# Gathering all rows first, and three 2 MB weight transfers per expert block instead of six of 1 MB

## The chip, the core and the metric

The kernel runs on one NeuronCore of a Trainium2 chip. The metric is the device time of one execution in microseconds (us). The core has five engines: TensorE (PE: matrix products, which accumulate in PSUM), VectorE (DVE), ScalarE (ACT), GpSimd (POOL) and SyncE (SP, which issues most transfers). They run side by side and wait for each other through semaphores. Sixteen DMA engines move data between HBM and the on-chip memory SBUF.

## The reference

One encoder block on 512 tokens of 1024 features, all in float32: a mixing part (differential attention, a conformer convolution, gates, an output projection) and then a mixture of experts. Only the second part changes:

```python
def hier_moe(h, w_rg, b_rg, w_re, b_re, w_g, w_u, w_d):
    # top-1 group of 8, then the top 2 of its 8 experts, for each of N = 512 tokens
    ...
    def expert_block(args):
        xb, e = args          # a block of rows that chose expert e
        return (jax.nn.silu(xb @ w_g[e]) * (xb @ w_u[e])) @ w_d[e]
    ...                       # weighted, summed into the tokens' rows
```

There are 64 experts. Each has w_g and w_u of 1024 x 512 and w_d of 512 x 1024, 2 MB apiece, so 6 MB of weights stand behind every block of rows. The 1024 choices (512 tokens, 2 each) are few beside that.

## The kernel before

The mixing part and the router take the first 420 us or so. After them the kernel runs one block of up to 64 rows after another (`BLK = 64`). Blocks 0 and 1 (`AHEAD = 2`) are written out and belong to experts 0 and 1, whose weights are loaded early; the rest is a loop whose count is read from `count_i`. With these inputs 62 blocks run, 60 of them in the loop.

A block works like this. `gather()` (L1382) picks the rows of the block: a one-hot matrix that DVE makes (`next_onehot`, L1098 to L1101) is multiplied with the normalized tokens `h2`, four tiles of 128 tokens, two matmuls each. DVE copies the result to `rows_sb` (L1120), PE transposes it (`transpose_rows`, L1389), and DVE copies it to `hTb` (L1122), the block's input. `block_products` (L1405) then multiplies it with gate and up weights in two halves of eight matmuls; the output's two halves of 64 partitions are computed side by side. ACT applies silu (L765), DVE multiplies (L1117), PE transposes the product (L1417), ACT copies it (L767), and PE multiplies it with the down weights in two halves of four matmuls (L1426). ACT copies the result to `y_sb` (L773) and POOL scatters it to HBM (L579).

The order is written out by hand. While block b is multiplied, block b + 1 is gathered: tiles 0 and 1 between the halves of gate and up, tile 2 behind them, tile 3 behind the transposes of the product, the transposes of the rows between the halves of down. So every one of the 62 blocks carries a whole gather.

The weights lie in two sets of six places of 1 MB (`weights`). Block b uses set b % 2. SP issues `load_sixth` (L487) in the order gate and up of half 0, gate and up of half 1, down half 0, down half 1. In the loop it waits, for each sixth, until PE has used what lies there (`gu_used` counts halves of gate and up, `down_used` counts blocks), and until the same sixth of the block before has landed (`in_w`). So at most one transfer of each sixth is under way. A run is what one partition takes in one piece of contiguous HBM: 8 KB for gate and up (four rows of 512), 4 KB for down (one row of 1024).

After the last block DVE reads the scattered rows back, adds them with their weights and normalizes, about 28 us.

## Time and profile before

| | us |
|---|---|
| median of 3 runs | 1401.41 (1401.35 to 1402.8) |
| the profiled execution | 1401.0 |
| its span, first to last instruction | 1399.2 |

| engine | busy us | share of the span |
|---|---|---|
| PE (matmul) | 1327.6 | 95% |
| DVE | 431.9 | 31% |
| ACT | 209.4 | 15% |
| POOL | 186.3 | 13% |

The transfers moved 435.78 MB, and SP's queue was busy for 76.1% of the time of 16 engines. Over the block loop, the last two thirds of the span, the page's slices show PE at nine tenths or more and the DMA engines at nine tenths or more with 413 to 418 GB/s. The profiled execution lies 1.8 us above its span and 0.4 us under the median. A share of busy time says which engine worked, not which one the others waited for; for that the waits and the order of time are needed. In the timelines an fp32 matmul shows as two records, so eight matmuls read x16.

### The profile page before, as it was taken

The page shows a single profiled execution, that of the slowest core. Times are in us where ns is not written, and L with a number is a line of the kernel's source. Part 1 is how long each engine was busy: PE and PEld are TensorE (multiplying, and loading weights), DVE is VectorE, ACT ScalarE, POOL GpSimd, SP SyncE. Part 2 cuts the span into 40 slices and gives each one's busy share as a digit, 9 for nine tenths or more (in the row PEclk, how much of TensorE's full clock was granted, in tenths as well). Part 3 has the DMA queues.
Part 4 walks back from the last instruction along what each step waited for, and adds up shares of the span by engine and source line. Part 5 has one row for each costly group of instructions (what it writes and reads, how often), then busy time and mean ns, then how long its engine had stood idle before and what let it go on. Part 6 is the DMA issues. An engine that isn't in the chain of part 4 may idle for free.

```text
span 1399.2 us, 17476 instructions
## 1 busy us (share of the span) xinstructions
PE 1327.6 (95%) x5883; PEld 580.5 (41%) x5883; DVE 431.9 (31%) x843; ACT 209.4 (15%) x453; POOL 186.3 (13%) x244
## 2 busy tenths in 40 slices
PE   5999988999979999999999999999999999999991
PEld 3878766744453333333333333333333333333330
DVE  4799344342334221121121122122112112112214
ACT  3232324430110100100000000010010000000002
POOL 2355433000000001001001001000100100100100
PEclk9999999999978999999999999999999999999996
DMA  5331311116145999999999999999999999999984
GB/s 208 115 121 61 121 60 57 68 57 251 49 180 219 386 417 416 417 417 417 416 418 417 415 417 417 415 416 417 416 417 417 413 414 410 415 414 415 416 339 186
DMA packets 93090, 435.78 MB, mean 311 GB/s; under 512 B 13488, under 2 KB 13517, under 8 KB 60810
## 3 DMA queue, kind: packets, MB, share of 16 engines
q1 hardware_dynamic: 86896, 429.23, 76.1%
q0 software_dynamic: 5312, 5.28, 1.2%
q10 hardware_dynamic: 858, 0.95, 0.2%
q8 instruction: 15, 0.25, 0.1%
q14 instruction: 9, 0.07, 0.0%
HBM read 429.10 MB, written 18.36 MB: 320 GB/s over the span
## 4 chain that ended last, share of the span: by engine, by line
issue 78%; PE 13%; POOL 2%; DVE 2%; DMA 2%; POOLq 1%; ACT 1%; ACTq 0%; DVEq 0%
PE ps_proj L1193 10%; PE ps_proj L1234 2%; POOL sb_tick L578 1%; POOL sb_tick L589 1%; DVE sb_x L1142 1%; DMA sb_weights<-in_w_in 1%; DMA sb_rb_sb<-in_rel_bias 1%; PE ps_scores L1248 1%; POOL expert_rows L579 0%; DVE sb_x L1152 0%; DVE sb_conv L932 0%; DMA sb_weights<-expert_rows 0%; POOL sb_weights_r L557 0%; PE ps_proj L1216 0%; PE ps_proj L1225 0%
## 5 line engine op out<-in xcount | busy, mean ns | idle before, releaser
L1405 PE MATMUL ps_proj<-sb_weights,sb_scratch 128*64 128x512 f32 x1984 | 446.9, 592 | 0.8 <-DVE sb_scratch L1107 0.8
L1405 PEld LDWEIGHTS ps_proj<-sb_weights,sb_scratch 128*64 128x64 f32 x1984 | 142.3, 137 | 283.2 <-issue 271.8
L1382 PE MATMUL ps_proj<-sb_hT,sb_scratch 128*64 128x512 f32 x1008 | 254.0, 605 | 0.0
L1426 PE MATMUL ps_scores<-sb_weights,sb_scratch 128*64 128x512 f32 x992 | 237.0, 598 | 0.0
L1117 DVE TENSOR_TENSOR sb_scratch<-sb_scratch,ps_proj 128x256 f32<-128x256 f32 x62 | 26.1, 421 | 536.0 <-ACT sb_scratch L765 536.0
L578 POOL TENSOR_TENSOR sb_tick<-sb_tick 1x1 f32<-1x1 f32 x62 | 11.6, 187 | 1013.9 <-ACT sb_scratch L773 1013.9
L1193 PE MATMUL ps_proj<-sb_hT_r,sb_weights_r 128*128 128x512 f32 x512 | 126.9, 401 | 2.7 <-POOL sb_weights_r L557 2.7
L1382 PEld LDWEIGHTS ps_proj<-sb_hT,sb_scratch 128*64 128x64 f32 x1008 | 67.4, 138 | 120.5 <-issue 120.5
L1426 PEld LDWEIGHTS ps_scores<-sb_weights,sb_scratch 128*64 128x64 f32 x992 | 65.3, 136 | 116.9 <-issue 90.3
L1193 PEld LDWEIGHTS ps_proj<-sb_hT_r,sb_weights_r 128*128 128x128 f32 x512 | 96.8, 192 | 30.5 <-issue 10.1
L765 ACT ACTIVATE sb_scratch<-ps_proj 128x256 f32<-128x256 f32 x62 | 23.8, 385 | 492.1 <-PE ps_proj L1405 492.1
L557 POOL TENSOR_TENSOR sb_weights_r<-sb_weights,sb_weights_r 128x1024 fp32r<-128x1024 f32 x36 | 86.0, 2404 | 76.4 <-ACT sb_weights_r L640 75.4
L773 ACT ACTIVATE sb_scratch<-ps_scores 128x512 f32 (+1 forms) x62 | 37.0, 598 | 318.6 <-PE ps_scores L1426 311.0
L1122 DVE COPY sb_scratch<-ps_proj 128x512 f32<-128x512 f32 x62 | 42.9, 692 | 99.5 <-PE ps_proj L1389 99.5
L1120 DVE COPY sb_scratch<-ps_proj 128x512 f32<-128x512 f32 x62 | 42.9, 691 | 96.1 <-PE ps_proj L1382 96.1
L579 POOL DMA_INDIRECT expert_rows<-sb_scratch,sb_idx x62 | 61.4, 991 | 32.3 <-issue 31.9
L1193 PE MATMUL ps_proj<-sb_x_r,sb_weights_r 128*128 128x512 f32 x256 | 63.2, 389 | 0.0
L1341 PE MATMUL ps_proj<-sb_weights 128*128 128x512 f32 x128 | 55.6, 593 | 0.0
L1193 PEld LDWEIGHTS ps_proj<-sb_x_r,sb_weights_r 128*128 128x128 f32 x256 | 48.1, 188 | 10.0
L1389 PEld LDWEIGHTS ps_proj<-sb_consts,sb_scratch 128*128 128x128 f32 x252 | 26.6, 142 | 52.1 <-issue 50.3
L1098 DVE TENSOR_TENSOR sb_scratch<-sb_small,sb_consts 128x512 f32<-128x512 f32 x62 | 43.0, 693 | 7.6 <-issue 1.2
L845 DVE SCALAR_TENSOR_TENSOR ps_scores<-sb_pad,sb_taps,ps_scores 128x512 f32<-128x512 f32 x58 | 42.5, 752 | 0.9
(221 smaller groups left out, 811.1 us busy)
## 6 DMA issues: line engine op xcount, KB each, us to landing
sb_weights<-in_w_exp_down SPq DMA_DIRECT2D x124, 1024.0 KB, 13.8
sb_weights<-in_w_exp_gate SPq DMA_DIRECT2D x124, 1024.0 KB, 14.0
sb_weights<-in_w_exp_up SPq DMA_DIRECT2D x124, 1024.0 KB, 15.2
sb_weights<-in_w_in SPq DMA_DIRECT2D x9, 2048.0 KB, 7.9
sb_x<-in_x SPq DMA_DIRECT2D x8, 512.0 KB, 9.2
sb_weights<-in_w_out SPq DMA_DIRECT2D x2, 2048.0 KB, 10.5
sb_weights<-expert_rows SPq DMA_DIRECT2D x4, 1024.0 KB, 7.9
sb_weights<-in_w_conv_pw SPq DMA_DIRECT2D x1, 2048.0 KB, 7.7
```

The source lines that it names most:

```text
L557: pool.tensor_tensor(w_low[name][:, :, j * P:(j + 1) * P], raw, high.bitcast(F32), ALU.subtract).then_inc(w_split, 1)
L579: pool.indirect_dma_start(out=y_dram, out_offset=bass.IndirectOffsetOnAxis(ap=idx[:, parity:parity + 1], axis=0), in_=y_sb[:, parity, :], ...
L773: act_e.activation(y_sb[:, of_parity(b), :].rearrange("p a s -> p (a s)"), ps_y, ACT.Copy)\
L845: dve.scalar_tensor_tensor(out=dst, in0=pad[:, c, k:k + SEQ], scalar=taps[:, c, k:k + 1], in1=conv_sum[c], op0=ALU.mult, op1=ALU.add).then ...
L1098: dve.tensor_tensor(hot_k, over(dest, BLK), pos8, ALU.is_equal).then_inc(loop_v, 1)
L1120: dve.tensor_copy(rows_sb, ps_rows[:, :]).then_inc(rows_ready, 1)
L1122: dve.tensor_copy(hTb, ps_hTb[:, :].rearrange("p (c s) -> p c s", s=P)).then_inc(hTb_ready, 1)
L1193: last = mm(dst[:, :], w[:, c, :], rows[:, c, :], start=i + c == 0, stop=i == 2 and c == KD - 1)
L1341: last = mm(dst[:, :], gates[:, c, t * P:(t + 1) * P], w[:, c, :], start=c == 0, stop=c == KD - 1)
L1382: last = mm(ps_rows[g * BLK:(g + 1) * BLK, :], onehot[:, t, :], h2[:, t, g * NW:(g + 1) * NW], start=t == 0, stop=t == T - 1)
L1405: last = mm(ps_gu[g * BLK:(g + 1) * BLK, :].rearrange("p (a n) -> p a n", a=2), hTb[:, c, half * BLK:(half + 1) * BLK], weights[:, place(p ...
L1426: last = mm(ps_y[g * BLK:(g + 1) * BLK, :], actT[:, j, half * BLK:(half + 1) * BLK], weights[:, place(parity, 4 + half), 2 * j + g, :], st ...
```

## The change

Three things change.

**Gathering.** The 1024 choices are gathered once, in expert order, in pieces of 64 that need not end where an expert's block ends: 16 pieces for the choices that are not in blocks 0 and 1's first 64 rows. They are written to a new buffer `hTs`, and block b takes its input as a slice of it from a position that DVE loads from `start_i`. Only the first 16 blocks carry a gather (`block_with_gather`, `GATHERED = 14` of them in the loop); all later ones (`block_products`) carry none. `sorted_places()` computes the positions in the first block: 18 more instructions on DVE and 2 more on PE (`rest_of_experts`).

**Order.** In a block with a gather, the piece's tiles are spread differently, the last two between the halves of gate and up, and the first two of the next piece later in the block.

**Weights.** `load_third` issues gate, up and down whole, 2 MB each: runs of 16 KB for gate and up, 8 KB for down. Each waits for both halves of gate and up, or for the block, to be used. The product's transposes read every second column, to fit the new order of down's rows. The buffers v_sb, conv, strip and pad become one tensor `work`, over which `hTs` lies.

```diff
-            def load_sixth(b, i, e):
-                dst = weights[:, place(b, i), :, :]
...
+            wd = ap("w_exp_down")[0].rearrange("e (h p j) n -> e p h (j n)", h=2, p=P)
+
+            def load_third(b, i, e):
+
+                dst = weights[:, place(b, 2 * i, 2), :, :]
+                if i < 2:
+                    sp.dma_start(dst.rearrange("p a c n -> p (a c n)"),
+                                 (wg, wu)[i][e].rearrange("e p n -> (e p) n")).then_inc(in_w[i], 16)
...
-                for sixth in range(6):
-                    if sixth in (0, 2):
-                        sp.wait_ge(gu_used, 2 * i + 1 + sixth // 2)
-                    if sixth == 4:
+                for third in range(3):
+                    if third == 0:
+                        sp.wait_ge(gu_used, 2 * i + 2)
+                    if third == 2:
                         sp.wait_ge(down_used, i + 1)
...
+            def rows_to_sorted(n, at):
+                dve.wait_ge(hTb_done, n)
+                dve.tensor_copy(hTs[:, at].rearrange("p (s g c) -> p c g s", g=2, c=4),
+                                ps_hTb[:, :].rearrange("p (c g s) -> p c g s", c=4, g=2)).then_inc(hTs_ready, 1)
+
+            def sorted_to_block(start):
+                dve.tensor_copy(hTb.rearrange("p c (g s) -> p c g s", g=2),
+                                hTs[:, bass.ds(start, BLK * KD)].rearrange("p (s g c) -> p c g s", g=2, c=4))\
+                    .then_inc(hTb_ready, 1)
...
+            dve.wait_ge(rows_done, 1)
+            block_onehot()
+            sorted_places()
+            prepare_slots()
+            gate_and_up(0)
+            copy_rows(2)
+            rows_to_block(2)
+            take_slots()
+            list_rows(0, slots[:, 0:1])
+
+            def block_with_gather(b, at, start, block_slots):
+                copy_rows(b + 2)
+                next_onehot(2 * b + 4, 2 * b + 5)
+                gate_and_up(b)
+                rows_to_sorted(b + 2, at)
+                dve.wait_ge(hTs_ready, b)
+                sorted_to_block(dve.value_load(start, min_val=0, max_val=2 * SEQ * KD))
+                list_rows(b, block_slots)
...
+            def first_block():
+                pe.wait_ge(hTb_ready, 1)
+                gate_up_half(0, 0, 0)
+                rest_of_experts()
+                pe.wait_ge(hot_b, 2)
+                gather([0, 1])
+                gate_up_half(0, 0, 1)
+                gather([2])
+                transpose_act(0)
+                gather([3])
+                pe.wait_ge(actT_ready, 1)
+                down_half(0, 0, 0)
+                pe.wait_ge(rows_ready, 2)
+                transpose_rows()
+                down_half(0, 0, 1)
+                slot_rows()
+                pe.wait_ge(hot_b, 3)
+                gather([0, 1])
```

The queue of SP in its loop, before (names are those of the code; `in_w0` to `in_w5` count landings of the six sixths):

```order
L522 ISA [waits gu_used]
L487 REGISTER_ALU [waits in_w0]
L487 DMA sb_weights<-in_w_exp_gate 128x2048
L487 ISA [waits in_w1]
L487 DMA sb_weights<-in_w_exp_up 128x2048
...
L487 ISA [waits in_w2,gu_used]
...
L487 ISA [waits in_w4,down_used]
L487 DMA sb_weights<-in_w_exp_down 128x2x1024
```

and of the change:

```order
L527 ISA [waits gu_used]
L493 REGISTER_ALU [waits in_w0]
...
L493 DMA sb_weights<-in_w_exp_gate 128x4096
L493 ISA [waits in_w1]
L493 DMA sb_weights<-in_w_exp_up 128x4096
...
L496 ISA [waits in_w2,down_used]
L496 DMA sb_weights<-in_w_exp_down 128x2x2048
```

Six transfers became three of twice the size, and one wait for half of gate and up is gone: the first of them now stands behind the whole.

PE in its loop, one block, before:

```order
L1405 MATMUL ps_proj<-sb_weights,sb_scratch 64x512 [waits in_w1,in_w0]
L1405 MATMUL ps_proj<-sb_weights,sb_scratch 64x512 x7
...
L1382 MATMUL ps_proj<-sb_hT,sb_scratch 64x512 [waits hot_b]
L1382 MATMUL ps_proj<-sb_hT,sb_scratch 64x512 x3
L1405 MATMUL ps_proj<-sb_weights,sb_scratch 64x512 [waits in_w3,in_w2]
...
L1382 MATMUL ps_proj<-sb_hT,sb_scratch 64x512 x2
L1417 MATMUL ps_aT<-sb_consts,sb_scratch 128x128 [waits act_ready]
...
L1426 MATMUL ps_scores<-sb_weights,sb_scratch 64x512 [waits in_w4,actT_ready]
...
L1389 MATMUL ps_proj<-sb_consts,sb_scratch 128x128 [waits rows_ready]
```

and one block of the change's second loop:

```order
L1480 ISA [waits hTb_ready]
L1484 MATMUL ps_proj<-sb_weights,sb_scratch 64x512 [waits in_w1,in_w0]
L1484 MATMUL ps_proj<-sb_weights,sb_scratch 64x512 x15
L1493 MATMUL ps_aT<-sb_consts,sb_scratch 128x128 [waits act_ready]
L1493 MATMUL ps_aT<-sb_consts,sb_scratch 128x128
L1501 MATMUL ps_scores<-sb_weights,sb_scratch 64x512 [waits in_w2,actT_ready]
L1501 MATMUL ps_scores<-sb_weights,sb_scratch 64x512 x7
```

The eight matmuls of the gather (L1382) and the four transposes (L1389) are gone from the block; nothing stands any more between the product's chain and what waits for it.

DVE in the first block of the change, between the one-hot (L1132) and the multiplication that the product's transposes wait for (L1162):

```order
L1132 TENSOR_TENSOR sb_scratch<-sb_scratch 128x256 [waits loop_v]
L1069 TENSOR_SCALAR sb_work<-sb_consts,sb_work 64x1
...
L1078 COPY sb_work<-ps_oT 128x64 [waits rest_done]
...
L1091 CAST sb_start_i<-ps_aT 1x80 [waits starts_done]
L1096 TENSOR_SCALAR sb_work<-sb_work 128x8 [waits link_v]
...
L1105 COPY sb_work<-sb_work 128x8x64 [waits link_v]
L1162 TENSOR_TENSOR sb_scratch<-sb_scratch,ps_proj 128x256 [waits gsig_ready]
```

Before, the rows from L1096 on (`prepare_slots`) followed the one-hot directly. The rows of `sorted_places`, L1069 to L1091, now stand ahead of them.

## Rows read from the trace of the kernel before

**Rows 1.** Timeline (start, us, engine, instructions): PE over one block.

```profile
810.65 3.60 PE L1405 MATMUL ps_proj<-sb_weights,sb_scratch 128*64 128x512 f32 x16
...
815.80 3.60 PE L1405 MATMUL ps_proj<-sb_weights,sb_scratch 128*64 128x512 f32 x16
...
820.34 0.44 PE L1417 MATMUL ps_aT<-sb_consts,sb_scratch 128*128 128x128 f32 x2
...
821.62 1.89 PE L1426 MATMUL ps_scores<-sb_weights,sb_scratch 128*64 128x512 f32 x8
...
823.44 0.66 PE L1389 MATMUL ps_proj<-sb_consts,sb_scratch 128*128 128x128 f32 x4
...
824.03 1.94 PE L1426 MATMUL ps_scores<-sb_weights,sb_scratch 128*64 128x512 f32 x8
...
825.79 3.60 PE L1405 MATMUL ps_proj<-sb_weights,sb_scratch 128*64 128x512 f32 x16
```

**Rows 2.** Windows: busy us of PE, PEld, DVE, ACT, POOL; clock, DMA share, GB/s.

```profile
480.00:1000.00 520.00, 517.20 (x2406) 172.97 (x2404) 103.87 (x238) 46.44 (x102) 46.49 (x104) 1.00 1.02 416
1000.00:1340.00 340.00, 338.11 (x1574) 113.11 (x1572) 69.17 (x159) 30.82 (x68) 29.73 (x66) 1.00 1.02 415
```

**Rows 3.** Waits of SP's queue, 480 to 780 us (total us, times, longest).

```profile
SPq L487 <- PE ps_scores L1426: 95.7, 19, 5.3
```

**Rows 4.** The same view, 1000 to 1350 us.

```profile
SPq L487 <- DMA sb_weights<-in_w_exp_up: 84.1, 45, 2.2
```

**Rows 5.** Timeline of SP's queue: two issues of the down weights, 22 blocks apart.

```profile
1007.94 2.70 SPq L487 DMA_DIRECT2D sb_weights<-in_w_exp_down  x2
...
1347.93 2.97 SPq L487 DMA_DIRECT2D sb_weights<-in_w_exp_down  x2
```

**Rows 6.** Windows in stretches of one run length, the columns of rows 2.

```profile
119.00:123.00 4.00, 4.00 (x19) 3.33 (x18) 4.00 (x7) 0.45 (x1) 0.00 (x0) 1.00 1.03 390
...
334.00:343.00 9.00, 9.00 (x22) 3.99 (x21) 2.29 (x4) 0.00 (x0) 0.00 (x0) 1.00 1.02 409
343.00:348.00 5.00, 5.00 (x13) 2.24 (x12) 0.69 (x1) 0.00 (x0) 0.00 (x0) 1.00 1.03 424
...
1378.00:1387.00 9.00, 0.00 (x0) 0.00 (x0) 6.54 (x6) 3.95 (x7) 0.00 (x0) 0.50 1.01 427
```

**Rows 7.** Timeline of PE: the end of block 0 and the start of block 1.

```profile
439.64 0.44 PE L1417 MATMUL ps_aT<-sb_consts,sb_scratch 128*128 128x128 f32 x2
...
445.19 2.01 PE L1375 MATMUL ps_scores<-sb_conv,sb_v_sb 128*128 128x80 f32 x16
447.13 3.23 PE L1405 MATMUL ps_proj<-sb_weights,sb_scratch 128*64 128x512 f32 x14
```

**Rows 8.** Timeline of DVE: one reduction, `prepare_slots` first and last, the next one-hot.

```profile
423.38 0.42 DVE L1058 TENSOR_REDUCE sb_strip<-sb_conv 128x4 f32<-128x256 f32 x1
...
430.89 0.16 DVE L1064 TENSOR_SCALAR sb_strip<-sb_strip 128x8 f32<-128x8 f32 x1
...
435.54 0.43 DVE L1073 COPY sb_v_sb<-sb_v_sb 128x512 f32<-128x512 f32 x1
...
448.74 0.42 DVE L1101 TENSOR_TENSOR sb_scratch<-sb_scratch 128x256 f32<-128x256 f32 x1
```

**Rows 9.** Timeline of DVE: its first work behind a load of a register.

```profile
463.57 0.69 DVE L1098 TENSOR_TENSOR sb_scratch<-sb_small,sb_consts 128x512 f32<-128x512 f32 x1 [1.25 <-issue]
```

**Rows 10.** The page's DMA issues: line engine op, size, median us to landing.

```profile
sb_weights<-in_w_in SPq DMA_DIRECT2D x9, 2048.0 KB, 7.9
```

**Rows 11.** Timeline of PE: the last matmuls of the last block.

```profile
1369.22 1.94 PE L1426 MATMUL ps_scores<-sb_weights,sb_scratch 128*64 128x512 f32 x8
```

**Rows 12.** Timeline of PE: the same transposes without and behind idle time (in brackets).

```profile
395.33 1.04 PE L1318 MATMUL ps_proj<-sb_consts,sb_hT 128*128 128x128 f32 x8
...
400.05 1.97 PE L1318 MATMUL ps_proj<-sb_consts,sb_hT 128*128 128x128 f32 x8 [1.94 <-DVE sb_hT L982]
```

251 lines of the change are left out of this document (156 added, 95 removed).

## The prediction

> **What bounds the kernel now.** I read the timeline of one block on PE first, since the page has PE at 95%. A block starts at 810.65 us and the next at 825.79: 15.14 us [rows 1]. Half of gate and up and the gather of two tiles, twelve matmuls, take 5.15 us, so a matmul takes 0.43 us. The gather's eight are 3.43 us of a block, its four transposes 0.59. PE stands only in the chain behind gate and up: its second half ends at 819.23, the transposes of the product start 1.11 us later, down 1.28 us after that, and gather matmuls fill most of both. PE is busy for 99.5% of the loop.
>
> That would promise 4 us in each of 46 blocks, some 180 us. But the same windows show the DMA engines at a share of 1.02 with 416 and 415 GB/s over 860 us [rows 2]: they are never idle either. The waits of SP's queue tell which of the two leads. Up to 780 us SP waits for PE to free a place [rows 3]; from about 1000 us on it waits for the landing of its own earlier transfers [rows 4]. So the transfers fall behind PE, and use up the lead they had. How slow they are when PE doesn't hold them is read from two issues of the same sixth, 22 blocks apart: (1347.93 - 1007.94) / 22 = 15.45 us for 6.29 MB [rows 5]. PE's period is 15.14, and PE ends on time only because of the lead. Two bounds lie 2% apart: taking work from PE lays the other bare.
>
> **The gather leaves 46 blocks.** By the prices of rows 1 a late block becomes 16 matmuls (6.86), 1.11, 1.28 and 8 matmuls (3.43): 12.68 us. Since 12.68 is under any period of the transfers that I can argue for, this gain is worth nothing beyond the step from PE's bound to theirs. PE then waits about 2.4 us a block for weights.
>
> A block with a gather has the same matmuls; one gather tile moves out of the place behind gate and up, where the row transposes now fill the gap, to between the halves of down: 5.15 + 3.43 + 1.11 + 1.28 + 1.72 + 0.86 + 1.72 = 15.27 us, against 15.14.
>
> **The transfers.** The period behind the loop's end is now the sum of bytes by their rate, and the rate depends on the run length. The queue's order tells which stretch moved which runs: w_in in 2 KB runs at 390 GB/s, x and down in 4 KB runs at 409, gate and up in 8 KB runs at 424, the scattered rows, read back in 8 KB runs, at 427 [rows 6]. Before: 4.194 MB at 425 and 2.097 MB at 409 are 9.87 + 5.13 = 15.00 us; the period has 0.45 more (scatters, completions). After: down has 8 KB runs, 4.93 us. For 16 KB there is no row. On one of 16 engines a run of 2, 4 and 8 KB takes 84, 160 and 308 ns, so two short runs cost 8 to 12 ns more than one of twice the length; with 10 ns a 16 KB run takes 607 ns, or 432 GB/s, and gate and up 9.71 us. The period is 9.71 + 4.93 + 0.45 = 15.09. Bounds: if 16 KB is no better than 8, 15.25; if the 0.45 halves with half as many transfers as well, 14.87; if neither length nor size matters, 15.45. I take 15.09, as three lengths of rows point one way.
>
> The Trainium skill (DMA: Bandwidth & Descriptors, Bandwidth, on small descriptors) gives a fixed cost of about 3 bus cycles per packet and finds joining worth it only up to 256 B. By it the estimate would be 0.8% off the period, 15.33, and a time of about 1405. Rows 6 disagree: from 4 to 8 KB they show 3.7% where the rule gives about 1%.
>
> Three transfers in place of six also make each wait coarser. In the steady state this costs nothing: a place of gate is free when block b's gate and up are multiplied, and is filled two blocks later, while up and down of the next block still stand in the queue. It costs at the start.
>
> **The start.** DVE's 18 new instructions stand ahead of `prepare_slots`, which stands ahead of the multiplication that PE's transposes wait for. Eight small ones at about 0.23 us bring DVE from 430.9 to 432.8; it then waits for PE's small product behind the first half (433.8); nine more take about 3.3 us at the pitch of the reductions (0.46 us for a large one) and 0.2 for the small, to 437.1. `prepare_slots` lasts from 430.89 to 435.97, or 5.1 us [rows 8], and so ends at 442.2, the multiplication at 442.6. PE's transposes start at 442.7 in place of 439.64, 3.05 us late [rows 7]. The slot matmuls then start at 448.25 and end at 450.2. New behind them: PE gathers two tiles before block 1, and waits for a one-hot that DVE makes only after it took the slots, which ended 2.0 us after the slot matmuls (449.16 against 447.13) [rows 7, 8]: 450.2 + 2.0 + 1.72 = 453.95. I add 1 us, since PE idles for some 2.6 us there and the clock may fall (rival D). Block 1 starts at 455, not 447.13: 7.8 us late.
>
> Its gate and up are used 8.58 us later, and SP issues block 3's gate at 464.2. Behind the other blocks nothing new is late: DVE loads a position (1.25 us idle at the one such load there is [rows 9]) and copies twice, at up to 1.06 each if strided access costs half again; it ends 4.5 us after the second half of gate and up, and PE needs it 6.7 us after in the first 16 blocks, against 3.4 and 5.8 in the rest. The extra 512-element memset on POOL is hidden by the first loads.
>
> **The sum.** Block 2 starts at 455 + 15.27 = 470.2; PE leads through block 15 (15.27 against 15.09), ends it at 684.1, finishes the last gather piece in 3.1 us, and uses block 16's gate and up at 694.1; SP issues block 18's gate at 694.7. From there 44 blocks at 15.09 are 664.0. Issue to first byte and last byte to landing are together 2.5 us: 2 MB land 7.9 us after issue [rows 10], of which 5.4 are bytes at 390 GB/s. The last down lands at 1361.2, its matmuls take 3.75: 1364.9. Before they end at 1371.2 [rows 11]. What follows is unchanged. So -6.2 us: 1401.0 - 6.2 = 1394.8 for a profiled execution, and with the 0.4 to the median **1395**.
>
> **Rivals.** With the same sum:
> - *A, 16 KB runs are no better than 8* (or are cut up, so that half of the change doesn't do what it says): 15.25. 694.7 + 671.0 + 2.5 + 3.75 = 1371.9, or +0.8: **1402**. For it: no row. Against: two steps of length each gained.
> - *B, the rate doesn't move*: the late rate is set by the memory and not by runs. For it: the loop's windows show 416 although a third of its bytes goes in 4 KB runs and the rest in 8. The period stays 15.45, the transfers lead from block 3 on: 464.2 + 59 x 15.45 + 6.25 = 1382.0, +10.9: **1412**, slower. The late start is the price, and it decides as soon as the period is over about 15.30.
> - *C, a run costs less than rows 6 say.* Their windows are 4 to 9 us long and hold other small traffic. If 32 fewer runs a block and engine save 3 ns each in place of 10, the period is 15.35 and the sum +5.0: **1406**. The skill's rule quoted above gives nearly this.
> - *D, TensorE's clock falls.* After only 1.94 us of idle time the same eight records of transposes took 1.97 us in place of 1.04 [rows 12], which is the lower of the two levels, 1.2 GHz. A late block has 2.4 us idle. A half of gate and up at that clock takes 3.43 us more, the block 16.1, or 1.0 over the period. Against it: such a block has no idle time left, so that the next one would run at full clock again. At every second block it is 22 x 1.0 = 22 us: **1417**.
> - *E, half the 0.45 goes too*: 14.87, 44 x 0.22 = 9.7 us less: **1385**.
> - That PE's saved 4 us a block come through is ruled out by the share of 1.02.
>
> **Chances.** Forecast 0.48, with a range of its own of 1390 to 1399; A 0.17; B 0.12; C 0.08; D 0.05; E 0.10. The range is **1385 to 1412**. It leaves out D and half of what lies beyond B and E. A measurement of this kernel can tell 0.2%, 2.8 us, from no change. Faster: the forecast but for its upper edge, E and a little of A and C, 0.60. Same: much of A and that edge, 0.16. Slower: B, C, D and the rest of A, 0.24.
>
> **What would show it.** Right: the busy time of PE in the late loop falls to some 75% with DMA at 1.02; issues of down 15.1 us apart; GB/s of 424 or more there; PE waits for landings of up weights in late blocks; the product's transposes of block 0 start about 3 us later; block 1 about 7 us later. Wrong: a period over 15.3 (A to C); a granted clock under 1.00 in the late loop (D); a block with a gather well over 15.3 us, from DVE's chain of load and copies; or idle DMA engines in the late loop, from the coarser waits.

## The result: 0.3% slower, and the profile after

The changed kernel takes 1406.72 us, the median of 8 runs (1403.65 to 1407.74), beside 1401.54 for the kernel before on the same chip. The ratio over all runs is 1.003, with a 95% interval of 1.002 to 1.0039 (the medians alone would give 1.0037). The forecast was 1395, some 6 us faster than before: the time went the other way, by 5.2 us. It lies inside the range of 1385 to 1412, but the range was drawn for the rivals, and none of them is what happened. The profiled execution took 1407.26 us, its span 1405.1. First the page: busy time by engine, and DMA packets.

```profile
PE 1190.1 (85%) x4987; PEld 548.3 (39%) x4987; DVE 363.0 (26%) x697; ACT 209.3 (15%) x453; POOL 186.4 (13%) x245
...
DMA packets 58370, 435.77 MB, mean 310 GB/s; under 512 B 10512, under 2 KB 10541, under 8 KB 26090
```

PE is busy for 137 us less than before and the kernel is slower. The windows (busy us of PE, PEld, DVE, ACT, POOL; clock, DMA share, GB/s) show that PE's work really left the late loop, with the DMA engines as full as before [rows 2]:

```profile
480.00:690.00 210.00, 205.05 (x962) 71.89 (x960) 54.58 (x112) 18.84 (x42) 17.57 (x39) 1.00 1.00 415
700.00:1000.00 300.00, 240.45 (x1020) 84.06 (x1018) 23.23 (x63) 28.63 (x63) 27.54 (x62) 0.96 1.00 421
1000.00:1340.00 340.00, 270.26 (x1128) 95.69 (x1130) 24.30 (x66) 30.00 (x66) 30.56 (x68) 0.95 1.01 421
```

PE falls from 99.4% to 79.5% of the last window, the rate rises from 415 to 421 GB/s. PE has idle time now and the DMA engines have none: the transfers set the pace. The waits of 700 to 1340 us (total us, times, longest) say the same:

```profile
PE ps_proj L1484 <- DMA sb_weights<-in_w_exp_up: 68.9, 40, 2.7
```

SP's queue, the first and the last of 41 issues of down, gives the period: (1354.67 - 748.86) / 40 = 15.145 us, where the forecast had 15.09 and [rows 5] had 15.45.

```profile
748.86 0.39 SPq L496 DMA_DIRECT2D sb_weights<-in_w_exp_down  x1
...
1354.67 0.39 SPq L496 DMA_DIRECT2D sb_weights<-in_w_exp_down  x1
```

So the main step of the forecast held, and something else ate more than it gave. The two places are the start and the end of the loop. PE at the start (start us, us, engine, instructions, idle time before), for [rows 7]:

```profile
431.93 3.65 PE L1484 MATMUL ps_proj<-sb_weights,sb_scratch 128*64 128x512 f32 x16 [0.78 <-DVE sb_scratch L1148]
...
444.74 0.51 PE L1493 MATMUL ps_aT<-sb_consts,sb_scratch 128*128 128x128 f32 x2 [2.42 <-DVE sb_scratch L1162]
445.18 1.98 PE L1456 MATMUL ps_proj<-sb_hT,sb_scratch 128*64 128x512 f32 x4
446.94 2.69 PE L1501 MATMUL ps_scores<-sb_weights,sb_scratch 128*64 128x512 f32 x8
...
456.03 3.28 PE L1456 MATMUL ps_proj<-sb_hT,sb_scratch 128*64 128x512 f32 x8 [2.01 <-DVE sb_scratch L1140]
459.15 3.60 PE L1484 MATMUL ps_proj<-sb_weights,sb_scratch 128*64 128x512 f32 x16
```

Block 1 starts 27.2 us after block 0 (459.15 - 431.93). Before it was 447.13 - 429.90 = 17.2 [rows 7]; this is where block 0 starts there:

```profile
429.90 3.65 PE L1405 MATMUL ps_proj<-sb_weights,sb_scratch 128*64 128x512 f32 x16 [0.78 <-DVE sb_scratch L1107]
```

The last two blocks of the change on PE:

```profile
1349.43 8.79 PE L1484 MATMUL ps_proj<-sb_weights,sb_scratch 128*64 128x512 f32 x32 [2.73 <-DMA sb_weights<-in_w_exp_up]
1359.14 0.51 PE L1493 MATMUL ps_aT<-sb_consts,sb_scratch 128*128 128x128 f32 x2 [0.93 <-DVE sb_scratch L1162]
1360.12 3.65 PE L1501 MATMUL ps_scores<-sb_weights,sb_scratch 128*64 128x512 f32 x16 [0.47 <-ACT sb_scratch L773]
1364.38 7.09 PE L1484 MATMUL ps_proj<-sb_weights,sb_scratch 128*64 128x512 f32 x32 [0.61 <-DMA sb_weights<-in_w_exp_up]
1372.40 0.50 PE L1493 MATMUL ps_aT<-sb_consts,sb_scratch 128*128 128x128 f32 x2 [0.93 <-DVE sb_scratch L1162]
1373.38 3.65 PE L1501 MATMUL ps_scores<-sb_weights,sb_scratch 128*64 128x512 f32 x16 [0.47 <-ACT sb_scratch L773]
```

The last block waits for **up**, not for down. Behind up's landing stand gate and up, the multiplication, the transposes with their copy, and down: 1377.03 - 1364.38 = 12.65 us. Down was there already: its matmuls wait for ACT's copy.

From one profile to the next the work ahead of block 0 varies by some us (block 0 starts between 424.9 and 432.7 in the profiles of this study, at 431.9 and at 424.9 in two profiles of the change itself), so profiles are compared from block 0's first gate and up to the end of the last down. After that end each kernel takes 27.9 to 28.2 us. From here on this stretch is called the **block stretch**: 1371.2 - 429.9 = 941.3 us before, 1377.0 - 431.9 = 945.1 in the change. So it holds 3.8 of the 5.2 us (2.3 in the second profile of the change, e1 below); the rest lies ahead of block 0, where it can't be told from the scatter.

### The profile page after: what moved, and what is told of

The parts are those of the page before. It is cut to its first block, busy times and chain, and to the rows that moved or that the text cites. A ratio compares the mean times of both kernels' runs of the same rounds, so it can differ in the third digit from the quotient of the medians.

```text
span 1405.1 us, 14917 instructions
## 1 busy us (share of the span) xinstructions
PE 1190.1 (85%) x4987; PEld 548.3 (39%) x4987; DVE 363.0 (26%) x697; ACT 209.3 (15%) x453; POOL 186.4 (13%) x245
## 2 busy tenths in 40 slices
DMA packets 58370, 435.77 MB, mean 310 GB/s; under 512 B 10512, under 2 KB 10541, under 8 KB 26090
## 4 chain that ended last, share of the span: by engine, by line
issue 78%; PE 14%; POOL 2%; DVE 2%; DMA 1%; POOLq 1%; ACT 0%; ACTq 0%; DVEq 0%
PE ps_proj L1267 11%; PE ps_proj L1308 2%; POOL sb_tick L584 1%; POOL sb_tick L595 1%; DVE sb_x L1216 1%; DMA sb_rb_sb<-in_rel_bias 1%; PE ps_scores L1322 1%; POOL expert_rows L585 0%; DVE sb_x L1226 0%; DVE sb_work L938 0%; DMA sb_weights<-expert_rows 0%; POOL sb_weights_r L563 0%; PE ps_proj L1290 0%; PE ps_proj L1299 0%; POOLq L602 0%
## 5 line engine op out<-in xcount | busy, mean ns | idle before, releaser
L1484 PE MATMUL ps_proj<-sb_weights,sb_scratch 128*64 128x512 f32 x1984 | 471.6, 628 | 73.7 <-DMA sb_weights<-in_w_exp_up 72.3
L1484 PEld LDWEIGHTS ps_proj<-sb_weights,sb_scratch 128*64 128x64 f32 x1984 | 165.9, 144 | 372.7 <-issue 371.7
L1501 PE MATMUL ps_scores<-sb_weights,sb_scratch 128*64 128x512 f32 x992 | 229.3, 599 | 21.8 <-ACT sb_scratch L773 21.8
L1162 DVE TENSOR_TENSOR sb_scratch<-sb_scratch,ps_proj 128x256 f32<-128x256 f32 x62 | 26.2, 422 | 640.3 <-ACT sb_scratch L771 640.3
L1267 PEld LDWEIGHTS ps_proj<-sb_hT_r,sb_weights_r 128*128 128x128 f32 x512 | 98.9, 196 | 31.2 <-issue 10.1
L771 ACT ACTIVATE sb_scratch<-ps_proj 128x256 f32<-128x256 f32 x62 | 23.8, 383 | 533.7 <-PE ps_proj L1484 533.7
L1456 PE MATMUL ps_proj<-sb_hT,sb_scratch 128*64 128x512 f32 x288 | 75.7, 631 | 2.0 <-DVE sb_scratch L1140 2.0
L1493 PE MATMUL ps_aT<-sb_consts,sb_scratch 128*128 128x128 f32 x124 | 31.4, 335 | 50.5 <-DVE sb_scratch L1162 49.6
L1493 PEld LDWEIGHTS ps_aT<-sb_consts,sb_scratch 128*128 128x128 f32 x124 | 19.6, 207 | 95.4 <-DVE sb_scratch L1162 95.4
L1144 DVE COPY sb_scratch<-ps_proj 128x512 f32<-128x512 f32 x18 | 12.5, 692 | 135.7 <-PE ps_proj L1456 135.7
L1156 DVE COPY sb_scratch<-sb_work 128x512 f32 x61 | 38.0, 624 | 32.1 <-issue 20.2
L851 DVE SCALAR_TENSOR_TENSOR ps_scores<-sb_work,sb_taps,ps_scores 128x512 f32<-128x512 f32 x58 | 42.4, 748 | 0.9
L1415 PEld LDWEIGHTS ps_proj<-sb_weights 128*128 128x128 f32 x128 | 24.2, 191 | 29.7 <-issue 29.6
```

The lines of the kernel that those rows point to most:

```text
L851: dve.scalar_tensor_tensor(out=dst, in0=pad[:, c, k:k + SEQ], scalar=taps[:, c, k:k + 1], in1=conv_sum[c], op0=ALU.mult, op1=ALU.add).then ...
L1156: dve.tensor_copy(hTb.rearrange("p c (g s) -> p c g s", g=2), hTs[:, bass.ds(start, BLK * KD)].rearrange("p (s g c) -> p c g s", g=2, c=4))\
L1267: last = mm(dst[:, :], w[:, c, :], rows[:, c, :], start=i + c == 0, stop=i == 2 and c == KD - 1)
L1415: last = mm(dst[:, :], gates[:, c, t * P:(t + 1) * P], w[:, c, :], start=c == 0, stop=c == KD - 1)
L1456: last = mm(ps_rows[g * BLK:(g + 1) * BLK, :], onehot[:, t, :], h2[:, t, g * NW:(g + 1) * NW], start=t == 0, stop=t == T - 1)
L1484: last = mm(ps_gu[g * BLK:(g + 1) * BLK, :].rearrange("p (a n) -> p a n", a=2), hTb[:, c, half * BLK:(half + 1) * BLK], weights[:, slice(6 ...
```

## Experiments

The theory after the first look: transfers set the late blocks, as forecast, and their gain is lost to a later start (block 16 begins late) and to a longer chain behind the last landing. Rivals: the transfers gain less than it seems, PE's lower clock costs time, and a coarser wait per transfer costs time. The results follow. Each kernel was timed beside the kernel before on the same chip, and the ratio, over all runs of both, is to that one: its median was 1399.35 us beside e1 to e4, 1401.19 beside e5 to e8 and 1402.42 beside e9 to e12, so times of different groups are compared by their ratios (periods: between issues of down over the last 40 blocks; `*` the transfers still use up their lead over PE there, and PE sets the end):

| kernel | us | ratio to before | 95% interval | block stretch | late period |
|---|---|---|---|---|---|
| the change | 1406.72 | 1.003 | 1.002 to 1.0039 | 945.1 | 15.145 |
| e1 the change again | 1404.74 | 1.0038 | 1.0021 to 1.0055 | 943.6 | 15.10 |
| e2 transfers only | 1404.41 | 1.0023 | 1.0005 to 1.004 | 945.3 | 15.21* |
| e3 gather only | 1411.05 | 1.0077 | 1.0053 to 1.0101 | 951.1 | 15.41 |
| e4 short runs | 1414.54 | 1.0095 | 1.0061 to 1.0129 | 956.6 | 15.37 |
| e5 start | 1402.77 | 1.002 | 1.0009 to 1.003 | 941.7 | 15.13 |
| e6 gate and up in halves | 1406.86 | 1.0036 | 1.0019 to 1.0053 | 945.7 | 15.30 |
| e7 e5 and e6 | 1402.63 | 1.0013 | 1.0002 to 1.0023 | 942.4 | 15.28 |
| e8 filled | 1408.63 | 1.0057 | 1.0037 to 1.0077 | 946.5 | 15.12 |
| e9 gate first | 1403.54 | 1.0005 | 0.9996 to 1.0015 | 941.4 | 15.13 |
| e10 e5 and e9 | 1398.5 | 0.9978 | 0.9966 to 0.9989 | 937.8 | 15.12 |
| e11 second start and e9 | 1395.04 | 0.9952 | 0.9938 to 0.9965 | 933.7 | 15.10 |
| e12 e2, product read plainly | 1401.19 | 0.9995 | 0.9986 to 1.0004 | 941.2 | 15.26* |

**e1, the change once more**, as a measure for the rest:

> The changed kernel itself, beside the others on the same chip. Theory S (start and tail): the transfers' period did fall as forecast, to 15.13 us in the late loop, and the loss comes from a late start (block 1 at 459 us, 12 us after before) and from the chain of the last block behind its last up weights (12.65 us). Expected: about 1406.5 us, period 15.1 in the late loop. Rival P (prelude): part of the 5 us is chance in the first 430 us (the profiled run reached the first gather 2.9 us later than before's). Then this profile reaches it within 1 us of before's, and the time would be nearer 1404.

1.0038 agrees with 1.003: the loss is real and small. Its block stretch is 1.5 us shorter than in the first profile, so differences under 2 us between single profiles mean nothing. All of the 1.5 us lie in block 0: block 1 starts 25.65 us after it, in place of 27.2. The last gather piece ahead of block 1 waited just as long as in the first profile, and ran at full clock this time:

```profile
448.74 1.94 PE L1456 MATMUL ps_proj<-sb_hT,sb_scratch 128*64 128x512 f32 x8 [2.01 <-DVE sb_scratch L1140]
```

In the change, e3, e4, e6, e8 and e9, whose first block is the same, block 1 starts 27.1 to 27.3 us after block 0. Rival P of the expectation is right in part: this profile reaches block 0 7 us earlier than the first, so single profiles scatter a good deal ahead of it. The medians, 5 us apart in both comparisons, don't hang on that.

### What the transfers are worth

**e2, the transfers alone.** The kernel before, with `load_third` and its waits, and the gather left in every block.

```diff
-                for sixth in range(6):
-                    if sixth in (0, 2):
-                        sp.wait_ge(gu_used, 2 * i + 1 + sixth // 2)
+                for third in range(3):
+                    if third == 0:
+                        sp.wait_ge(gu_used, 2 * i + 2)
...
-                    last = pe.transpose(ps_actT[:, c * P:(c + 1) * P], act[:, c * P:(c + 1) * P], ident)
+                    last = pe.transpose(ps_actT[:, c * P:(c + 1) * P], act_jf[:, c, :], ident)
```

> The kernel before with the three 2 MB transfers alone (16 KB and 8 KB runs), every block still with its gather. Theory S: PE's period stays 15.14 and bounds, the transfers at 15.1 no longer fall behind (issue to landing stays under 15 us), so the time is that of before, 1401.5, within 1.5 us. Rival W (coarser waits cost): waiting for both halves before gate is reloaded starves PE or the DMA engines, and the time is 3 us or more above before.

1.0023: slower, by 3 to 4 us, where PE should have gone on at its own period; the expectation missed. Two things could do it: the coarser waits, or a part of the edit that I had costed at nothing, the transposes of the product that now read every second column. The groups by line (busy us, mean ns of one) say the latter, first e2, then the kernel before:

```profile
L1413 PE MATMUL ps_aT<-sb_consts,sb_scratch 128*128 128x128 f32 x124 | 31.4, 335 | 5.1
```

```profile
L1417 PE MATMUL ps_aT<-sb_consts,sb_scratch 128*128 128x128 f32 x124 | 27.2, 301 | 5.1
```

4.2 us more over 62 blocks, all on PE's path, and PE waits no longer than before. The Trainium skill (SBUF — State Buffer, the note on cachelines in Door 1: The DMA port swizzle) has it that a read is at full speed as long as two accesses fall in each line of 16 bytes, and that up to 4 fp32 can be strided for free. Every second fp32 column is two per line. By that rule it would be free; this trace disagrees, with 0.51 us in place of 0.44 for a pair.

**e12, the same with the product read plainly**, to tell the two apart. Down goes in 4 KB runs again, still 2 MB a transfer, and the coarse waits stay.

```diff
-            wd = ap("w_exp_down")[0].rearrange("e (h p j) n -> e p h (j n)", h=2, p=P)
+            wd = ap("w_exp_down")[0].rearrange("e (j p) n -> e p j n", p=P)
...
-                    last = pe.transpose(ps_actT[:, c * P:(c + 1) * P], act_jf[:, c, :], ident)
+                    last = pe.transpose(ps_actT[:, c * P:(c + 1) * P], act[:, c * P:(c + 1) * P], ident)
```

> e2_transfers_only (the gather as before, three transfers of 2 MB) with down in 4 KB runs as before, so that the product's transposes read contiguous columns again; gate and up stay in 16 KB runs. Theory S2 (e2 was slower than the kernel before because the transposes with a stride take 0.51 us in place of 0.44 in every one of 62 blocks that PE leads, 4.3 us): transposes back at 0.44, block at 15.14, time that of the kernel before within 1 us, ratio 1.000. Rival W (the coarser waits cost it): the block stays 15.21 and the time at e2's, ratio 1.002.

The group of transposes of e12:

```profile
L1413 PE MATMUL ps_aT<-sb_consts,sb_scratch 128*128 128x128 f32 x124 | 27.2, 301 | 5.0
```

0.9995, and a block stretch of 941.2 for 945.3 in e2: the stride was the loss of e2, and three coarse waits in place of six cost nothing where PE leads. And with faster transfers PE still sets the end, at its own 15.14 us.

**e3, the gather alone**: the change with `load_sixth` as before (six transfers of 1 MB, runs of 8 and 4 KB, product read plainly).

```diff
-                for third in range(3):
-                    if third == 0:
-                        sp.wait_ge(gu_used, 2 * i + 2)
-                    if third == 2:
+                for third in range(6):
+                    if third in (0, 2):
+                        sp.wait_ge(gu_used, 2 * i + 1 + third // 2)
+                    if third == 4:
                         sp.wait_ge(down_used, i + 1)
```

> The change without its transfers: six of 1 MB in 8 KB and 4 KB runs, gathering over 16 blocks. Theory S: late period 15.45 as before's late one; the transfers lead nearly from the start, 59 x 15.45, and the last block's chain is 9.4 us behind its last half of up: about 1410. Rival R (the rate does not hang on runs and transfers): the late period is 15.13 here too and the time about 1403.

1.0077, the block stretch 951.1. It lays bare what six transfers really take, with PE out of the way: (1357.37 - 741.05) / 40 = 15.41 us. That agrees with the 15.45 that the forecast read while PE and the transfers were nearly tied [rows 5]. SP's queue in e3:

```profile
741.05 2.95 SPq L497 DMA_DIRECT2D sb_weights<-in_w_exp_down  x2
...
1357.37 2.99 SPq L497 DMA_DIRECT2D sb_weights<-in_w_exp_down  x2
```

**e4, three transfers of 2 MB with the short runs** (8 and 4 KB), so that number and run length come apart.

```diff
-            wg = ap("w_exp_gate")[0].rearrange("e (p r) f -> e p (r f)", p=P)
+            wg = ap("w_exp_gate")[0].rearrange("e (h p r) f -> e p h (r f)", p=P, h=2)
...
-            wd = ap("w_exp_down")[0].rearrange("e (h p j) n -> e p h (j n)", h=2, p=P)
+            wd = ap("w_exp_down")[0].rearrange("e (j p) n -> e p j n", p=P)
```

> The change with its three transfers of 2 MB, but each in the runs of before: 8 KB for gate and up, 4 KB for down (the rows of gate and up come in another order, so that the products are of wrong rows; sizes and order of work are the same). Tells run length from number of transfers. If the run length makes the rate: late period 15.4, time about 1416. If the number of transfers does: late period 15.15 and about 1407. Halfway would be 15.27 and 1410.

e4 leaves out the match between the rows of gate and up and the block's input, so its products are not those of the reference. Sizes, waits and order of work are those of the change. Its period is 15.37 us, from the same two issues:

```profile
747.26 0.38 SPq L496 DMA_DIRECT2D sb_weights<-in_w_exp_down  x1
...
1362.06 0.38 SPq L496 DMA_DIRECT2D sb_weights<-in_w_exp_down  x1
```

Longer runs gain 0.23 us a block (15.37 to the change's 15.145). Half as many transfers gain 0.04 at most: kernels with the change's own transfers scatter from 15.10 to 15.145, so 0.04 can't be told from nothing. It is the run length. And e4 loses 5.5 us of block stretch to e3 although its period is shorter: whole transfers have a price elsewhere.

**e6, gate and up in halves again** (1 MB, 8 KB runs), down whole: five transfers.

```diff
+                if i < 4:
+                    dst = weights[:, place(b, 2 * (i % 2) + i // 2), :, :]
+                    sp.dma_start(dst.rearrange("p a c n -> p (a c n)"),
+                                 (wg, wu)[i % 2][e, i // 2].rearrange("e p n -> (e p) n")).then_inc(in_w[i], 16)
...
-                    if third == 0:
-                        sp.wait_ge(gu_used, 2 * i + 2)
+                    if third in (0, 2):
+                        sp.wait_ge(gu_used, 2 * i + 1 + third // 2)
```

> The change with gate and up in halves of 1 MB (8 KB runs, five transfers a block), down whole. Theory S: PE can start on the first half, so the chain behind the last up transfer is 9.4 in place of 12.65 us (-3.3), and the first half is reloaded 3.4 us earlier; the period rises from 15.13 to about 15.2 (+3 over 44 blocks): about 1403. Rival R (16 KB runs matter most): period 15.3 and about 1407.

(1359.14 - 747.23) / 40 = 15.30 us, as rival R of the expectation had it; the expected 15.2 us and 1403 did not come. With e3 and the change that splits the gain: down from 4 to 8 KB is worth 0.11 us a block (15.41 to 15.30), gate and up from 8 to 16 KB 0.15. Both steps hold a part of the 0.04 above, since down became one transfer in the first, and gate and up two in place of four in the second.

The pages show that the runs of 16 KB were not cut up. The change has 58370 packets, this run 76228:

```profile
DMA packets 76228, 435.79 MB, mean 310 GB/s; under 512 B 12497, under 2 KB 12526, under 8 KB 28075
```

The difference of 17858 is 62 blocks of 288 and 2 more: 256 runs fewer (2 x 128 partitions), and 16 for each of the two transfers fewer.

Yet e6 takes the time of the change: 44 blocks at 0.15 are 6.6 us more, and 6.0 come back (945.7 against the first profile's 945.1, with the same start). Of those, 3.4 lie where the transfers take the lead: SP issues block 18's gate 265.4 us after block 0's start in e6 and 268.8 in the change, because it waits for half of block 16's gate and up only. The rest is of the size of what the end saves. Its last rows on PE:

```profile
1368.98 3.65 PE L1486 MATMUL ps_proj<-sb_weights,sb_scratch 128*64 128x512 f32 x16 [1.33 <-DMA sb_weights<-in_w_exp_up]
1373.57 0.51 PE L1495 MATMUL ps_aT<-sb_consts,sb_scratch 128*128 128x128 f32 x2 [0.93 <-DVE sb_scratch L1165]
1374.55 3.65 PE L1503 MATMUL ps_scores<-sb_weights,sb_scratch 128*64 128x512 f32 x16 [0.47 <-ACT sb_scratch L776]
```

Only 9.2 us stand behind the last landing of up there, in place of 12.65.

### The end

**e9, gate first.** This changes the chain behind up without touching the transfers. In the blocks without a gather PE multiplies the whole gate when it has landed and up behind it, into another PSUM bank, and silu runs beside up. ACT then waits for the gate alone, and DVE reads up from the other bank (both left out below).

```diff
+            def gate_then_up(b, parity):
+                for m in range(2):
+                    pe.wait_ge(in_w[m], 16 * b + 16)
+                    for half in range(2):
+                        for c in range(4):
+                            for g in range(2):
+                                last = mm((ps_gu, ps_rows)[m][g * BLK:(g + 1) * BLK, 0:256],
...
             def block_products(b, parity):
                 pe.wait_ge(hTb_ready, b + 1)
-                gate_up_half(b, parity, 0)
-                gate_up_half(b, parity, 1)
+                gate_then_up(b, parity)
```

> In the 46 blocks without a gather PE multiplies the whole gate first, as soon as it has landed, and up behind it, each into a PSUM bank of its own (matmuls of 256 columns in place of 512); ACT's silu runs beside up, and only the multiplication on DVE waits for up. Theory T (the end is late because PE's chain behind the last up landing is 12.65 us: both products 6.86, 1.16, transposes and copy 0.98, down 3.65): now some 3.5 of up, 0.6, 0.98 and 3.65 stand behind it, 8.7 us, so down's matmuls end about 4 us earlier after the last down issue, and the time is 1406.7 - 4.0 = 1402.7, ratio to the kernel before 1.001. The period of the late blocks stays 15.13. Rival U (the end follows the last landing of down, or a matmul of 256 columns costs over 0.15 us more than half of one of 512, which fills PE's idle time): no gain or a loss, 1406 to 1410.

1403.54, ratio 1.0005 [0.9996, 1.0015] against the change's 1.003 [1.002, 1.0039]: better by some 3.5 us, with a block stretch 3.7 us shorter than the first profile's (block 1 starts at the same 27.2 us) and the same period. Its last block:

```profile
1359.62 3.67 PE L1552 MATMUL ps_proj<-sb_weights,sb_scratch 128*64 128x256 f32 x32 [1.15 <-DMA sb_weights<-in_w_exp_gate]
1364.53 3.67 PE L1552 MATMUL ps_proj<-sb_weights,sb_scratch 128*64 128x256 f32 x32 [1.23 <-DMA sb_weights<-in_w_exp_up]
1368.82 0.50 PE L1497 MATMUL ps_aT<-sb_consts,sb_scratch 128*128 128x128 f32 x2 [0.61 <-DVE sb_scratch L1211]
1369.90 3.65 PE L1505 MATMUL ps_scores<-sb_weights,sb_scratch 128*64 128x512 f32 x16 [0.58 <-DMA sb_weights<-in_w_exp_down]
```

Now down's matmuls wait for down's landing, 5.4 us after up's, and the end is that landing and 3.65 us: the tail that the forecast had assumed for the change. In the change 12.65 us stood behind up's landing, here 5.37 + 3.65 = 9.02. So 3.6 us of the miss are this. The expectation had put 8.7 us of PE's own work behind up; it is down's landing that ends last.

### The start

DVE in the first block of the change. The 18 new instructions end at 439.2, with 1.39 us of waiting for PE's small product among them, `prepare_slots` runs from 439.27 to 444.3, and only then comes the multiplication (L1162) that PE waits for:

```profile
432.84 0.20 DVE L1069 TENSOR_SCALAR sb_work<-sb_consts,sb_work 64x1 f32<-64x1 f32 x1
...
435.98 0.23 DVE L1078 COPY sb_work<-ps_oT 128x64 f32<-128x64 f32 x1 [1.39 <-PE ps_oT L1474]
...
439.02 0.22 DVE L1091 CAST sb_start_i<-ps_aT 1x80 int32<-1x80 f32 x1
439.27 0.17 DVE L1096 TENSOR_SCALAR sb_work<-sb_work 128x8 f32<-128x8 f32 x1
...
444.27 0.41 DVE L1162 TENSOR_TENSOR sb_scratch<-sb_scratch,ps_proj 128x256 f32<-128x256 f32 x1
```

**e5.** Two moves in DVE's order: the multiplication of block 0 ahead of `prepare_slots`, and the one-hot of the next piece ahead of the slots.

```diff
             sorted_places()
+            gate_and_up(0)
             prepare_slots()
-            gate_and_up(0)
             copy_rows(2)
+            next_onehot(4, 5)
             rows_to_block(2)
...
-            dve.wait_ge(rows_done, 2)
-            next_onehot(4, 5)
```

> The change with two moves in DVE's first block: the multiplication of block 0 ahead of prepare_slots, and the next one-hot ahead of taking the slots. Theory S: the product's transposes of block 0 start 2.4 us earlier and PE does not idle 2.0 us before the gather ahead of block 1, so block 1 starts 4 to 6 us earlier, and all of it reaches the end, since PE leads the first 16 blocks and the transfers follow: 1401 to 1402.5. Rival: the transfers are late anyway and the start hides, 1406.

Ratio 1.002 [1.0009, 1.003] against 1.003 and 1.0038 of the change: by the times alone they do not come apart. The profiles say more. PE no longer waits for the multiplication (0.15 us); it now waits 2.36 us for the rows' copy behind `prepare_slots`, and block 1 starts 23.8 us after block 0. That is 3.4 us earlier than in the first profile and 1.8 earlier than in e1, and the block stretch is 3.4 and 1.9 us shorter. What is gained at the start reaches the end.

**e7, e5 and e6 together:**

> Both edits together. If they add: about 1398 to 1399, below before. If the transfers lead from the first block on, less than the sum: 1401.

1402.63, block stretch 3.3 us under that of e6 and 0.7 over that of e5. The expected 1398 to 1399 did not come, since it counted a gain of e6 that e6 alone did not show. The start is worth the same with either form of transfer.

**e10, e5 and gate first together**, to see if start and end add up:

> e5_start and e9_gate_first together. If the two misses (start and tail) add up: 1402.8 - 4.0 = 1398.8, ratio 0.998. If the earlier start only feeds idle time that gate first removes, no better than either, 1402.7.

1398.5 for 1398.8 expected, and 0.9978 [0.9966, 0.9989] against e9's 1.0005 [0.9996, 1.0015] on the same chip: they add up, the start is worth 4 to 5 us there (3.5 of block stretch), and this version is faster than the kernel before.

**e11, a second start, with gate first.** `prepare_slots` is cut in three and laid where DVE waits anyway.

```diff
             sorted_places()
-            prepare_slots()
+            prepare_first()
             gate_and_up(0)
+            prepare_second()
             copy_rows(2)
+            prepare_third()
             rows_to_block(2)
+            next_onehot(4, 5)
             take_slots()
```

> As e10, and DVE's preparation of the slots is cut in three and laid into the idle stretches of the first block (three instructions before the multiplication, three before the copy of the rows, three behind it), the one-hot of the next piece behind them. PE's transposes of the rows no longer wait (2.36 us in e5_start); block 1 should start about 450.6 in place of 454.7, 4 us earlier. Theory S (every us at the start reaches the end, because the transfers lead without a gap from block 16 on and start that much earlier): 1398.8 - 4.0 = 1394.8, ratio 0.995, faster than both kernels. Rival: the transfers lead already in the first blocks, and the gain of the start stops at about 1 us: 1398.

1395.04, ratio 0.9952 [0.9938, 0.9965]: 0.5% faster than the kernel before, and by the ratios 0.8% faster than the change. PE no longer waits in block 0, and the matmuls that had slowed down there take their full-clock times:

```profile
443.21 0.51 PE L1502 MATMUL ps_aT<-sb_consts,sb_scratch 128*128 128x128 f32 x2
443.65 1.08 PE L1465 MATMUL ps_proj<-sb_hT,sb_scratch 128*64 128x512 f32 x4
...
450.77 1.94 PE L1465 MATMUL ps_proj<-sb_hT,sb_scratch 128*64 128x512 f32 x8
452.54 3.60 PE L1493 MATMUL ps_proj<-sb_weights,sb_scratch 128*64 128x512 f32 x16
```

Block 1 starts 19.9 us after block 0, 7.3 us earlier than in the change. The rival, that the transfers lead already and cap the gain at 1 us, falls: block stretch 4.1 under that of e10.

### The clock

Late blocks of the change come in pairs: a slow gate and up (8.79 us, behind 2.73 us of idle time), then a quick one (7.09, behind 0.61). That is rival D's mechanism. **e8** fills the idle time with four more matmuls in each late block, whose result nobody reads.

```diff
             def block_products(b, parity):
                 pe.wait_ge(hTb_ready, b + 1)
+                for t in range(2):
+                    for g in range(2):
+                        mm(ps_rows[g * BLK:(g + 1) * BLK, :], onehot[:, t, :], h2[:, t, g * NW:(g + 1) * NW],
+                           start=t == 0, stop=t == 1)
```

> The change with four matmuls of 1.7 us more in each of the 46 late blocks, ahead of gate and up, into an unused bank (extra work, same result). Theory S: PE's idle time in the late loop is free, so the time stays at 1406.5 within 1.5 us although PE has 79 us more to do, and the granted clock there rises from 0.95 to 1.00. Rival K (the fallen clock costs): the time falls by 2 us or more. Rival M (PE is near the bound): it rises by 5 us or more.

The last window of e8:

```profile
1000.00:1340.00 340.00, 290.80 (x1304) 103.05 (x1302) 24.32 (x66) 30.41 (x67) 31.10 (x69) 1.00 1.01 422
```

The granted clock is 1.00 there, and the kernel is not faster: 1.0057 [1.0037, 1.0077] against 1.0038 [1.0021, 1.0055] for e1 and 1.003 [1.002, 1.0039] for the change, and the late period is 15.12 against 15.10 and 15.15. So the lower clock did not lengthen the change's loop. The other side of it: some 79 us of extra matmuls (46 x 1.72) cost 1.4 us of block stretch against the first profile, or 3 to 4 us by the ratios, more than the 1.5 us expected. The 1.4 us are where PE still leads: with the filler ahead of block 16, SP issues block 18's gate 270.4 us after block 0's start, in place of 268.8.

e9 shows the clock at 1.00 without any filler:

```profile
1000.00:1340.00 340.00, 257.56 (x1840) 134.85 (x1842) 25.42 (x69) 30.38 (x67) 29.74 (x66) 1.00 1.01 422
```

So does e6, which has the same matmuls as the change and more idle time:

```profile
1000.00:1340.00 340.00, 254.01 (x1108) 87.06 (x1110) 24.29 (x66) 30.04 (x66) 29.74 (x66) 1.00 1.01 417
```

In e6 the idle time of a block comes in four pieces (1.33, 1.33, 0.93 and 0.47 us), in the change's slow blocks as 2.73 us in one piece, 0.93 and 0.47.

## Where the prediction was right and where it was wrong

Both are counted from block 0's start, 429.9 in the forecast and 431.9 in the profile. These 2.0 us lie ahead of block 0, where two profiles of the change itself differ by 7.

| step | forecast | measured | miss |
|---|---|---|---|
| product's transposes of block 0 | 12.8 | 12.8 | 0 |
| block 1 starts | 25.1 | 27.2 | 2.1 |
| block 16 starts | 257.3 | 261.2 | 3.9 |
| SP issues block 18's gate | 264.8 | 268.8 | 4.0 |
| last landing of down | 931.3 | 937.8 (from e9's distance of up and down) | 6.5 |
| end of the last down | 935.0 | 945.1 | 10.1 |

- **Both bounds, right.** Taking the gather from PE gave nothing beyond the step to the transfers' bound. e3 is the proof: gather out, transfers as before, 0.8% slower.
- **The transfers' period, right in size.** 15.09 forecast, 15.10 to 15.15 measured: two runs of 8 KB do gain from being one of 16 KB. Rivals A and C, at 15.25 and 15.35, fall; so does B, since the rate moved. Split by e3, e4 and e6, the gain was put together a little wrongly: down's longer runs were to bring 0.20 us and bring 0.11 at most, gate and up's 0.16 and bring 0.15 at most, as 0.04 or less of the two together comes from the number of transfers. Rival E wanted 0.22 from that number. By the estimate from the Trainium skill's rule of 3 cycles a packet (DMA: Bandwidth & Descriptors, Why small descriptors are slow) the period was to be 15.33; the runs show a larger gain than that.
- **Two signs were not met.** The rate in the late loop was to be 424 GB/s or more and is 421. PE's share there was to fall to some 75% and fell to 79.5%; at the full clock of e6 it is 74.7%.
- **DVE's chain at the start, right to 0.1 us** up to the transposes (12.81 against 12.8). Some of that is luck: behind the wait it counted nine instructions in 3.3 us, and there are ten, from 435.98 to 439.24. **The clock there, mis-sized.** I added 1 us; the rows show 1.98 in place of 1.08, 2.69 in place of 1.89 and 3.28 in place of 1.94, together 3.0, all behind 2.0 to 2.4 us of idle time, as rival D's row had it for the transposes [rows 12]. Miss: 2.1 us. In e1, with the same idle time, it is 1.5 less, so the size of this term changes from one execution to the next.
- **The block with a gather, mis-sized by 0.06.** 15.33 against 15.27, the strided read of the product; e3, which reads it plainly, has 15.26. The stride had been put at nothing without a reason. Over 15 blocks that is 0.9 us, and in e2, where PE leads throughout, it is the whole loss.
- **The last piece of the gather**: 4.0 us in place of 3.1. PE idles 0.79 and 0.62 us there that I had not counted: the first for a copy, the second by the code for a register load, which the view doesn't name.
- **44 late blocks**: 2.5 us, mostly 44 x 0.05.
- **The tail, the step that failed.** "The last down lands at 1361.2, its matmuls take 3.75" took down for the last thing waited for because it is issued last, although the forecast itself named PE's waits for up as a sign of being right. Up's landing has the longer chain behind it: 12.65 us against 9.0 by way of down. In the kernel before PE led, and this didn't show. The price is 3.6 us, shown by e9. It is the one wait that the forecast had wrong, but it alone does not turn a gain into a loss: with it the forecast would have been some 1398.6. The other terms that were too small, above all the clock at the start and the late blocks, did the rest.
- **A price that the forecast ruled out**: "in the steady state this costs nothing". True of the coarser waits in the loop, and of those where PE leads (e12). At the one place where the lead changes hands, block 16 to 18, waiting for both halves in place of one costs 3.4 us; it stood in the sum as a time without being seen as a price, and e6 shows it. The DMA engines stand idle there for a moment: their share is 0.87 from 700 to 710 us of the change, 0.99 in the 10 us before and 1.01 in the 10 us after.
- **Rival D**: the clock did fall in every second late block, and cost nothing there. Its sum took a slow block for a late one; but PE's lateness of one block is taken out of the idle time of the next, and the transfers, which set the period, do not wait for it. Its place was the start, where PE has no slack.

The sum: 4.0 at the start and up to block 18, 2.5 in the blocks, 3.6 at the end, 2.0 ahead of block 0, which with 0.3 or 0.4 of rounding and ends makes up the 12.5 us from 1394.8 to 1407.26. Against the kernel before, medians 5.2 us apart: the transfers' gain is real (e3 to the change, 951.1 to 945.1, even with 3.4 and 3.6 us of price in it), but the start costs more than it is worth, and with the start and the end mended the same idea is 0.5% faster than before (e11).

Open: how the 3.4 us at the change of lead and gate first would go together was not tried. Nor was the strided read removed without giving up down's 8 KB runs. And e4's 5.5 us over e3 are explained by e6's two terms (3.4 and 3.6, less 1.6 of period) only to the size, not by a run of its own. Why the matmuls behind 2.01 us of idle time ahead of block 1 ran slowly in six of seven profiles and not in e1 is not shown, nor what makes the work ahead of block 0 vary by 7 us.

## What to carry to other kernels

When the bound passes from an engine to the transfers, the last transfer issued need not be the last one waited for: for each landing add up what stands behind it, and order the work so that the chain behind the last ones is short. A gain per block is worth no more than the lateness it starts from; every us on the path before the loop came through in full here (e10 against e9: block 1 starts 3.4 us earlier, the stretch is 3.5 shorter; e11 against e10: 3.9 and 4.1), so new work there belongs in the idle stretches of its engine. A change of layout that comes along with longer runs has a price at the reader: find the instruction that reads it, and price the stride.

## What the runs showed of the hardware

- **Runs of 16 KB beat runs of 8 KB.** In a loop set by the transfers, 6.29 MB took 15.41 us (gate and up 8 KB, down 4 KB), 15.30 (8 and 8) and 15.10 to 15.15 (16 and 8): 408, 411 and 415 to 417 GB/s. Half as many transfers at the same runs: 15.37 for 15.41, which is within the scatter of single profiles.
- **A strided fp32 read slows a transpose.** Two transposes of 128x128, reading every second column, take 0.51 us in place of 0.44, at the same full clock (e2 and e12).
- **A gate and up in 32 matmuls of 256 columns takes as long as in 16 of 512** where nothing is waited for: 7.08 us at 705.46 us of e9, against 7.04 at 709.06 us of e8, both without idle time before them. Cut in two by the wait for up it is 3.67 us twice, against 7.09. The busy time of weight loads rose from 95.7 to 134.9 us in the last window, some 1.7 us a block, and nearly all of that is hidden beside matmuls.
- **In these runs the clock went with how the idle time is cut, and not with how much there is.** Some 3.7 to 3.9 us of idle time a block in four pieces, none over 1.45 us (e9 and e6): granted clock 1.00. Some 3.1 us a block on the mean, but 2.7 us of it in one piece ahead of gate and up in every second block (the change): 0.95 over the window, with the gate and up behind that piece at 8.79 us for 7.09. Ahead of block 1, a piece of 2.01 us was followed by slow matmuls (3.3 us for 1.94) in six of seven profiles, and by full speed in e1.
